# A hybrid encoder layer with routed experts: router product in column groups, and the order of work around the routing

## Chip, core and metric

The kernel runs on one core of a Trainium2 chip. The metric is the device time of one launch in microseconds (us), as the median of several runs. TensorE, VectorE, ScalarE, GpSimd and SyncE (which here only issues transfers) each run a stream of their own and are ordered by semaphores. Every tensor is float32.

## What is computed

Two sequences (256 and 1024 tokens, width 1024) go through two layers with shared weights. Each layer adds a mix of windowed attention, a bidirectional state space scan and a bidirectional mLSTM, and then a mixture of 16 experts, in which each expert chooses its tokens. The change touches the part from the output projection to the first expert:

```python
x = x + jnp.concatenate([ya, yb, yc], axis=-1) @ w_out[l]
h = _rmsnorm(x, ffn_norm[l])
aff = jax.nn.softmax((xf @ router).astype(jnp.float32), axis=-1)   # (T, 16)
gate, idx = lax.top_k(aff.T, cap)          # cap = 128 (sample), 32 (prompt)
xs = xf[idx]
hid = jax.nn.silu(einsum('ecd,edf->ecf', xs, w_gate)) * einsum('ecd,edf->ecf', xs, w_up)
ye = einsum('ecf,efd->ecd', hid, w_down) * gate[..., None]
out = zeros.at[idx.reshape(-1)].add(ye.reshape(-1, D))
```

## The kernel before, in words

The 1280 tokens are 10 blocks of 128 (`NC`), taken in `ORDER`: the eight of the sample first, then the two of the prompt (`NP`). A loop over layers (`Fori`) holds one block in which each engine's program is written out by hand; the order of lines is the order of work on that engine. A helper (`link`) adds a semaphore step to an instruction and has its own engine wait for it, so VectorE and ScalarE run strictly one instruction after the other. On TensorE all products go through `mm` (L1474) and on VectorE most operations through `tt` and `ts` (L984, L988), so rows are told apart by their tiles and shapes. A float32 product is two records in the trace.

**The passes.** TensorE runs `for n in range(1, NC + 1)` (L1870 on). Pass n makes the output projection of block n in two halves of eight products each (`out_proj(n, hf, i0, i1)`: 128x512, the weights of w_out moving), and in between the attention of later blocks (`scores`, `turn_p`, `turn_y`), the transposes of the normalized block n-1 (`turn_h2`, into PSUM bank 3) and its router product (`logits`, L1820). VectorE adds the projection to x (`add_x`), copies the transposed halves to `H2T` (`keep_h2`, for the last two blocks on ScalarE), and makes a softmax of the logits in two steps: `route_shift` (maximum and subtraction) and, after ScalarE's exponential `route_exp`, `route`. ScalarE also squares x, scales it by the root that GpSimd makes, and takes the attention's exponentials (`attn_exps`). The eight products of `logits` have a block of H2T (128x128) stationary and 16 columns of the router moving.

**The rounds.** When the eight sample blocks are routed, TensorE transposes their affinities into bank 7 (`aff_turned`, L1907), VectorE copies them to `AFF` (32 rows, one per expert and half of the sequence, 512 columns) and takes the eight best of every row 16 times (`best_eight`: MAX8, FIND_INDEX8, MATCH_REPLACE8; `rounds(lo, hi)`). The last two blocks (prompt) are still being projected meanwhile, and their adds, shifts and scalings are set between the rounds by hand. The last four rounds take the prompt's 16 rows too, after a second turn of affinities.

**Towards the experts.** `top_done` lets TensorE turn the lists so that each partition has its token's index; `keep_clock(6, 8)` issues eight products that nobody reads; GpSimd gathers the prompt's tokens of four experts (`gather_quad(0)`) and the sample's of the first (`gather(0)`), TensorE transposes them (`turn_quad`, `turn_tokens`), and VectorE copies them with the norm's gain into `XT` (`copy_quad`, `spread_quad`, `copy_tokens`; `g_copied` counts the half blocks). Then the loop over e starts with `EG` and `EU` (gate and up).

**SyncE's queue.** After the last stores it issues `down_load(0)`, then for e from 1 `gate_up_load(e)` and `down_load(e)`; each of these is 2 MB a tensor, and from e = 2 on they wait for the buffer of expert e-2.

**Parameters** sit in one tile `part`, in the order of the table `PAR`; `router` is 8 x 16 columns and stands last. `FOLD` (made on VectorE at the start of a layer, L1013) has 32 columns; column e sums the partitions p with p mod 32 = e. It is used by the gates of the mixers, whose products already stand in four column groups.

## Time and profile before

| what | us |
|---|---|
| runs | 2566.73, 2566.39, 2561.0 |
| median | 2566.39 |
| profiled execution | 2561.19 |
| its span in the trace | 2559.5 |
| TensorE busy | 2393.1 (93%) |
| VectorE busy | 1041.7 (41%) |
| ScalarE busy | 560.6 (22%) |
| GpSimd busy | 528.4 (21%) |

The span runs from the first to the last instruction of the profiled execution; the time around it is 1.7 us. The shares are means over stages that have different limits. A layer takes roughly half of the span, and its passes lie at 600 to 780 us and 1870 to 2050 us, the rounds at 780 to 821 and 2051 to 2092, the experts behind them. A row of a timeline has the start, the time, engine, line, operation, tiles, shape and count, and in brackets the idle time before it with what ended it. Matmul records overlap, so the start of the next row, not the sum of durations, tells what a group costs.

### The profile page before, as it was taken

To read this page: it belongs to the slowest core of one execution; us is meant where nothing else is said; L and a number is where in the kernel's file an instruction comes from. 1 tells how busy PE (TensorE), PEld (TensorE's weight loads), DVE (VectorE), ACT (ScalarE), POOL (GpSimd) and SP (SyncE) were. 2 spreads that over 40 slices of the span, in tenths; PEclk is the share of its full clock that TensorE was granted. 3 is DMA by queue.
4 is the path that set the end of the run, shared out by engine and by line. 5 is a ranking of instruction groups with operands and counts; after the bars stand their busy time and mean duration, and the time that the engine had idled before them with its cause. 6 is when DMAs were issued, how large, how long until landed. Compare 5 with 4: busy or idle time off the path is not lost. (4 is left out here: it accounts for less than half of the span.)

```text
span 2559.5 us, 34127 instructions
## 1 busy us (share of the span) xinstructions
PE 2393.1 (93%) x13478; PEld 1733.6 (68%) x13478; DVE 1041.7 (41%) x1990; ACT 560.6 (22%) x1202; POOL 528.4 (21%) x544
## 2 busy tenths in 40 slices
PE   5999998998996999999869999999989969999997
PEld 3567577874554887887635675778745548878876
DVE  3672345487537111111138524455865371111111
ACT  3220223243331111111132202323333211111110
POOL 1002444143211111211110114531332001111111
PEclk8999999999997999999989999999999979999999
DMA  6010322121227687887331012211212276788782
GB/s 219 19 34 17 99 83 70 63 84 66 72 74 261 212 277 262 298 269 260 104 121 36 17 43 89 88 61 59 91 50 75 75 271 228 258 292 286 250 291 65
DMA packets 149654, 357.61 MB, mean 140 GB/s; under 512 B 9981, under 2 KB 38273, under 8 KB 149410
## 3 DMA queue, kind: packets, MB, share of 16 engines
q1 hardware_dynamic: 134514, 313.42, 34.4%
q0 software_dynamic: 14976, 41.95, 6.6%
q8 instruction: 110, 1.80, 0.3%
q14 instruction: 54, 0.44, 0.1%
HBM read 313.06 MB, written 47.52 MB: 141 GB/s over the span
## 5 line engine op out<-in xcount | busy, mean ns | idle before, releaser
L1474 PE MATMUL ps<-MID,HT 128*128 128x512 f32 (+1 forms) x2176 | 595.1, 495 | 4.3 <-PE ps L1474 3.2
L1474 PE MATMUL ps<-HT,MID 128*128 128x160 f32 (+1 forms) x4192 | 583.9, 307 | 7.2 <-DVE HT L984 2.9
L1474 PEld LDWEIGHTS ps<-HT,MID 128*128 128x128 f32 (+1 forms) x4192 | 563.0, 189 | 25.9 <-issue 25.6
L1474 PE MATMUL ps<-RING,HT 128*128 128x256 f32 (+2 forms) x2080 | 475.1, 397 | 9.3 <-ACT MID L791 4.6
L1474 PEld LDWEIGHTS ps<-RING,HT 128*128 128x128 f32 (+1 forms) x2080 | 377.1, 193 | 98.2 <-issue 43.8
L1474 PEld LDWEIGHTS ps<-MID,HT 128*128 128x128 f32 (+1 forms) x2176 | 231.5, 152 | 225.7 <-issue 209.2
L1474 PE MATMUL ps<-HT,RING 128*128 128x512 f32 (+1 forms) x960 | 354.1, 526 | 3.1 <-ACT MID L785 2.5
L993 DVE SCALAR_TENSOR_TENSOR HT<-HT,ps 128x160 f32<-128x160 f32 x128 | 41.1, 321 | 712.0 <-ACT HT L970 712.0
L1474 PEld LDWEIGHTS ps<-HT,RING 128*128 128x128 f32 x960 | 180.9, 191 | 164.1 <-issue 156.4
L741 POOL DMA_INDIRECT y_sample<-SCR,idxs x32 | 50.6, 1581 | 745.5 <-ACT SCR L977 745.5
L970 ACT ACTIVATE HT<-ps 128x160 f32<-128x160 f32 x128 | 38.9, 304 | 593.7 <-PE ps L1474 593.7
L984 DVE TENSOR_TENSOR HT<-ps,part 128x512 f32<-128x512 f32 (+1 forms) x180 | 113.7, 632 | 65.7 <-PE ps L1488 22.7
L608 POOL TENSOR_TENSOR SCR<-MID,small 128x512 f32<-128x512 f32 x32 | 39.7, 1242 | 344.6 <-DVE MID L984 274.3
L984 DVE TENSOR_TENSOR SCR<-SCR,ps 128x512 f32<-128x512 f32 x80 | 55.0, 687 | 130.6 <-POOL SCR L622 95.7
L1474 PE MATMUL ps<-MID 128*64 128x128 f32 (+3 forms) x1136 | 101.0, 312 | 4.4 <-DVE RING L988 2.3
L1474 PEld LDWEIGHTS ps<-MID 64*128 64x128 f32 (+1 forms) x1136 | 75.8, 175 | 36.8 <-issue 26.0
L984 DVE TENSOR_TENSOR SCR<-SCR,small 128x1024 f32<-128x1024 f32 (+1 forms) x60 | 59.3, 989 | 95.3 <-POOL SCR L617 94.7
L1474 PE MATMUL ps<-MID,SCR 128*128 128x65 f32 (+1 forms) x640 | 79.4, 277 | 11.7 <-DVE TMP L984 11.7
L975 ACT ACTIVATE SCR<-ps,small 128x512 f32<-128x512 f32 x64 | 44.0, 687 | 201.6 <-PE ps L1474 201.6
L1474 PEld LDWEIGHTS ps<-MID,SCR 128*128 128x128 f32 x640 | 74.4, 191 | 17.6 <-issue 14.8
L677 POOL TENSOR_TENSOR SCR<-SCR,small 128x1536 f32<-128x1536 f32 (+1 forms) x20 | 48.1, 2406 | 177.8 <-DVE small L1281 177.6
L984 DVE TENSOR_TENSOR TMP<-MID,small 128x256 f32<-128x256 f32 (+1 forms) x64 | 26.9, 420 | 140.3 <-PE ps L1474 139.2
(212 smaller groups left out, 2183.0 us busy)
## 6 DMA issues: line engine op xcount, KB each, us to landing
MID<-w_gate SPq DMA_DIRECT2D x32, 2048.0 KB, 8.6
MID<-w_up SPq DMA_DIRECT2D x32, 2048.0 KB, 14.1
MID<-w_down SPq DMA_DIRECT2D x32, 2048.0 KB, 14.7
RING<-w_in SPq DMA_DIRECT2D x22, 1024.0 KB, 5.3
SCR<-cs_rows SPq DMA_DIRECT2D x20, 1024.0 KB, 5.2
SCR<-m_rows SPq DMA_DIRECT2D x20, 512.0 KB, 4.0
MID<-y_sample SPq DMA_DIRECT2D x16, 512.0 KB, 7.6
MID<-w_out SPq DMA_DIRECT2D x8, 1024.0 KB, 6.4
```

Of the source, the lines that this page charges most:

```text
L608: link(pool.tensor_tensor(DXS[:, n % 2, d, :].rearrange("p (h e) -> p h e", h=SH), XS[:, c, :].rearrange("p (h e) -> p h e", h=SH), WS[:, ...
L677: link(pool.tensor_tensor(v, v, ADEN[n % 2].unsqueeze(2).to_broadcast([P, AH, nk * P]), ALU.mult), pn_made)
L741: pool.indirect_dma_start(ys[:, :], bass.IndirectOffsetOnAxis(ap=idxs[:, e:e + 1], axis=0), YO[e % 2], None, compute_op=ALU.add, bounds_ch ...
L970: link(act.activation(THG, ps[:, 2 + f % 2, 0:TOK], ACT.Tanh, scale=0.5), gate_tanh)
L975: link(act.mul(YO[e % 2][:, hf * 512:(hf + 1) * 512], ps[:, 4 + hf, :], gts[:, e:e + 1]), down_scaled)
L984: link(dve.tensor_tensor(out, a, b, op), to)
L993: link(dve.scalar_tensor_tensor(out=out, in0=a, scalar=x, in1=b, op0=op0, op1=op1), to)
L1474: return pe.matmul(out, a, b, start=start, stop=stop)
```

## The change

It has five parts.

1. `logits` has the router's columns stationary and H2T moving, product k in column group k mod 4 (32 columns each, the 16 of the router and 16 that follow it, so that `router` moves to the front of `PAR`). Four partial sums lie in 4 x 32 partitions. ScalarE copies them to the tile `LGP`, and `fold_logits` multiplies LGP with 16 columns of FOLD, which gives the logits in the old shape and place.
2. In the passes, `logits(n - 1)` stands ahead of `turn_y(n + 1, 2)`, the fold after the fifth product of the second half, and in pass 8 the last product of the projection comes after the transposes for AFF.
3. VectorE's rounds are cut into a pick and a drop, the add of block 8 goes behind the first pick, and the shifts and scalings of the prompt's blocks are placed anew. The memset of AFF's unused part is moved ahead of the passes.
4. SyncE waits for the first two gathers before `down_load(1)`.
5. `keep_clock` has five products for eight, and the first expert's first products start with half of the tokens' copies.

```diff
-for _name, _w in (("gmix", 8), ..., ("dskip", 8), ("router", 128)):
+for _name, _w in (("router", 128), ("gmix", 8), ..., ("dskip", 8)):
+ROUTER = PAR["router"][0]
+        LGP = VO[:, 1664:1664 + P]
@@ SyncE
                 for e in range(1, E):
                     gate_up_load(e)
+                    if e == 1:
+                        sp.wait_ge(quad_gathered[0], 16)
+                        sp.wait_ge(gathered[0], 16)
                     down_load(e)
@@ ScalarE
+                def keep_logits(c):
+                    act.wait_ge(lg_parts, c + 1)
+                    if c >= 1:
+                        act.wait_ge(lg_made, c)
+                    link(act.copy(LGP, ps[:, 3, 0:P]), lg_kept)
...
                     if n >= 1:
+                        keep_logits(n - 1)
                         route_exp(n - 1)
@@ VectorE
-                def best_eight(r):
+                def pick_eight(r):
+                    rows, v8, places = ranked(r)
                     link(dve.max(v8, rows))
-                    link(dve.max_index(idxus[0:n, 8 * r:8 * r + 8], v8, rows))
-                    if r < CAPS // 8 - 1:
-                        link(dve.match_replace(rows, v8, rows, -1.0))
+                    link(dve.max_index(places, v8, rows))
+                def drop_eight(r):
+                    rows, v8, places = ranked(r)
+                    link(dve.match_replace(rows, v8, rows, -1.0))
...
-                link(dve.memset(AFF[2 * E:3 * E, SEQS[0]:512], -1.0))
-                add_x(NC - 2, 1)
                 dve.wait_ge(aff_turned, 1)
                 link(dve.tensor_copy(AFF[0:2 * E, :], ps[0:2 * E, 7, :]))
-                rounds(0, 3)
+                pick_eight(0)
+                add_x(NC - 2, 1)
+                drop_eight(0)
+                rounds(1, 4)
                 take_x(NC - 1)
-                rounds(3, 5)
+                rounds(4, 6)
                 route_shift(NC - 2)
-                rounds(5, 6)
+                pick_eight(6)
                 route(NC - 2)
+                drop_eight(6)
                 add_x(NC - 1, 1)
-                rounds(6, 10)
+                rounds(7, 10)
+                pick_eight(10)
                 route_shift(NC - 1)
-                rounds(10, 11)
+                drop_eight(10)
                 route(NC - 1)
                 rounds(11, PROMPT_ROUND)
@@ TensorE
-                pe.wait_ge(fold_made, 1)
                 def logits(c):
                     pe.wait_ge(h2t_copied, 2 * c + 2)
                     for k in range(KD):
-                        last = mm(ps[:, 3, 0:E], H2T[:, k, :], pr("router")[:, k * E:(k + 1) * E], k == 0, k == KD - 1)
-                    last.then_inc(lg_made, 1)
+                        j = k % 4
+                        last = mm(ps[32 * j:32 * j + 32, 3, 0:P], part[:, ROUTER + k * E:ROUTER + (k + 2) * E], H2T[:, k, :], k < 4, k >= 4)
+                    last.then_inc(lg_parts, 1)
+                def fold_logits(c):
+                    pe.wait_ge(lg_kept, c + 1)
+                    mm(ps[:, 3, 0:E], LGP, FOLD[:, 0:E]).then_inc(lg_made, 1)
...
                     out_proj(n, 1, 1, 3)
+                    logits(n - 1)
                     if n + 1 < NC:
                         turn_y(n + 1, 2)
-                    out_proj(n, 1, 3, 4)
-                    logits(n - 1)
-                    out_proj(n, 1, 4, 8)
+                    out_proj(n, 1, 3, 5)
+                    fold_logits(n - 1)
+                    out_proj(n, 1, 5, 7)
                     if n == NC - 2:
                         pe.wait_ge(aff_made, NC - NP)
...
                         last.then_inc(aff_turned, 1)
+                    out_proj(n, 1, 7, 8)
...
-                keep_clock(6, 8)
+                keep_clock(6, 5)
...
-                    pe.wait_ge(g_copied, turn_at(e, 1) + 1)
+                    pe.wait_ge(g_copied, turn_at(e, 1) + (1 if e else 0))
...
                             for k in range(KD):
+                                if n == 0 and (at, k) == (0, KD // 2):
+                                    pe.wait_ge(g_copied, turn_at(0, 1) + 1)
```

## Rows read from the trace of the kernel before

**Rows 1.** Busy time by stretch (us, PE, PEld, DVE, ACT, POOL, clock, DMA share, GB/s), one pass.

```profile
712.70:733.68 20.98, 20.82 (x96) 11.16 (x95) 8.53 (x19) 6.71 (x18) 2.17 (x3) 1.00 0.21 75
```

**Rows 2.** Timeline, VectorE, rounds of layer 2: copy, two maxima, cast after the last.

```profile
2051.45 0.68 DVE L1399 COPY TMP<-ps 32x512 f32<-32x512 f32 x1
2052.16 0.68 DVE L1355 MAX8 TMP<-TMP 32x8 f32<-32x512 f32 x1
...
2054.44 0.68 DVE L1355 MAX8 TMP<-TMP 32x8 f32<-32x512 f32 x1
...
2091.82 0.17 DVE L1415 CAST TMP<-idxus 16x32 f32<-16x32 uint32 x1
```

**Rows 3.** Timeline, `keep_clock` in both layers, token copies and first expert product.

```profile
824.15 6.82 PE L1474 MATMUL ps<-cstt 128*128 128x384 f32 x16
...
2094.67 8.14 PE L1474 MATMUL ps<-cstt 128*128 128x384 f32 x16
...
2105.13 1.42 DVE L984 TENSOR_TENSOR HT<-ps,part 128x512 f32<-128x512 f32 x2
2106.65 14.95 PE L1474 MATMUL ps<-HT,MID 128*128 128x160 f32 x96 [1.17 <-issue]
```

**Rows 4.** Timeline of a pass in layer 1 around `logits`, all engines.

```profile
707.94 0.69 DVE L1337 COPY HT<-ps 128x512 f32<-128x512 f32 x1
...
708.27 1.88 PE L1474 MATMUL ps<-MID,HT 128*128 128x512 f32 x4
...
709.80 0.20 ACT L922 ACTIVATE small<-small 128x4 f32<-128x4 f32 x1
...
710.08 1.53 PE L1474 MATMUL ps<-MID 128*64 128x128 f32 x24
...
712.70 1.85 PE L1474 MATMUL ps<-part,HT 128*128 128x16 f32 x16
...
714.41 5.40 PE L1474 MATMUL ps<-MID,HT 128*128 128x512 f32 x12
...
726.76 0.37 ACT L930 COPY MID<-ps 128x256 f32<-128x256 f32 x1 [3.50 <-PE ps L1757]
```

**Rows 5.** Groups of TensorE records by shape, whole span: count | busy, mean ns.

```profile
L1474 PE MATMUL ps<-MID,HT 128*32 128x256 f32 x1024 | 61.9, 382 | 0.0
...
L1474 PE MATMUL ps<-MID 128*64 128x128 f32 x416 | 28.9, 289 | 2.3 <-DVE RING L988 2.3
```

**Rows 6.** Timeline, end of pass 8 in layer 1: routing, transposes, copy to AFF.

```profile
775.97 0.18 DVE L1342 TENSOR_REDUCE small<-ps 128x1 f32<-128x16 f32 x1 [2.42 <-PE ps L1474]
...
777.12 0.23 DVE L988 TENSOR_SCALAR TMP<-MID,small 128x16 f32<-128x16 f32 x1
...
779.23 0.60 PE L1907 MATMUL ps<-cstt,TMP 128*32 128x128 f32 x4
...
780.23 0.68 DVE L1399 COPY TMP<-ps 32x512 f32<-32x512 f32 x1
```

**Rows 7.** Timeline, layer 1: the last add, the last logits, the last shift.

```profile
796.34 0.69 DVE L984 TENSOR_TENSOR RING<-ps,RING 128x512 f32<-128x512 f32 x1
...
803.26 3.59 PE L1474 MATMUL ps<-part,HT 128*128 128x16 f32 x16 [0.75 <-ACT HT L935]
...
806.96 0.17 DVE L1342 TENSOR_REDUCE small<-ps 128x1 f32<-128x16 f32 x1 [0.82 <-PE ps L1474]
```

**Rows 8.** First gathers: two issues (timeline), then their time to landing (transfers by window).

```profile
825.67 0.96 POOL L717 DMA_INDIRECT HT<-h_sample,idxs  x1 [0.85 <-DVE idxs L984]
...
2094.11 1.08 POOL L723 DMA_INDIRECT HT<-h_prompt,idxg  x1 [23.63 <-DVE idxg L1421]
...
HT<-h_sample,idxs POOLq DMA_INDIRECT x1, 5.0
...
HT<-h_prompt,idxg POOLq DMA_INDIRECT x1, 4.4
```

**Rows 9.** Busy time by stretch as in rows 1, one microsecond after expert 0's start.

```profile
2107.00:2108.00 1.00, 1.00 (x6) 1.00 (x5) 0.00 (x0) 0.00 (x0) 0.00 (x0) 0.50 0.07 16
```

More of the change, by code:

```diff
@@ L27 @@
 _n = 0
-for _name, _w in (("gmix", 8), ("gffn", 8), ("gy", 8), ("convw", 30), ("convb", 6), ("qg", 1), ("kg", 1),
-                  ("sink", 4), ("gbias", 32), ("alog", 16), ("dskip", 8), ("router", 128)):
+for _name, _w in (("router", 128), ("gmix", 8), ("gffn", 8), ("gy", 8), ("convw", 30), ("convb", 6), ("qg", 1), ("kg", 1),
+                  ("sink", 4), ("gbias", 32), ("alog", 16), ("dskip", 8)):
     PAR[_name] = (_n, _n + _w)
@@ L343, in program @@
         scaled_odd = layer_sem("scaled_odd")
-        fold_made = layer_sem("fold_made")
         softplus_exp = layer_sem("softplus_exp")
@@ L410, in program @@
         lg_made = layer_sem("lg_made")
+        lg_parts = layer_sem("lg_parts")
+        lg_kept = layer_sem("lg_kept")
         h2t_copied = layer_sem("h2t_copied")
@@ L1009, in scale_x @@
                     ts(XN[c], XN[c], rs[:, c:c + 1], None, ALU.mult, to=scaled_odd)
-                link(dve.tensor_reduce(out=FOLD, in_=ident.rearrange("p (j e) -> p e j", j=4), axis=AX, op=ALU.add), fold_made)
+                link(dve.tensor_reduce(out=FOLD, in_=ident.rearrange("p (j e) -> p e j", j=4), axis=AX, op=ALU.add))
                 ts(NSINK, pr("sink"), -1.0, None, ALU.mult)
@@ L1349, in route, with ranked @@
                     ts(AFTM[:, j, g * E:(g + 1) * E], AFT, rec[:, 0:1], None, ALU.mult, to=aff_made)
-                def best_eight(r):
+                def ranked(r):
                     n = 3 * E if r >= PROMPT_ROUND else 2 * E
-                    rows, v8 = AFF[0:n, :], VALS[0:n, 8 * r:8 * r + 8]
+                    return AFF[0:n, :], VALS[0:n, 8 * r:8 * r + 8], idxus[0:n, 8 * r:8 * r + 8]
+                def pick_eight(r):
+                    rows, v8, places = ranked(r)
                     link(dve.max(v8, rows))
-                    link(dve.max_index(idxus[0:n, 8 * r:8 * r + 8], v8, rows))
-                    if r < CAPS // 8 - 1:
-                        link(dve.match_replace(rows, v8, rows, -1.0))
+                    link(dve.max_index(places, v8, rows))
+                def drop_eight(r):
+                    rows, v8, places = ranked(r)
+                    link(dve.match_replace(rows, v8, rows, -1.0))
                 def rounds(lo, hi):
                     for r in range(lo, hi):
-                        best_eight(r)
+                        pick_eight(r)
+                        if r < CAPS // 8 - 1:
+                            drop_eight(r)
                 def take_x(n):
@@ L1374, in _ @@
                 attn_den(2)
+                link(dve.memset(AFF[2 * E:3 * E, SEQS[0]:512], -1.0))
                 for n in range(1, NC - 1):
```

## Prediction

> **What bounds the kernel now.** I read three views in this order. The busy table by stretch comes first, for one pass of the loop over n: TensorE works 20.82 of 20.98 us at the full granted clock of 1.00, that is at 2.4 GHz, while VectorE has 8.53 and ScalarE 6.71 [rows 1]. So the passes are bound by TensorE, and what it sheds there is gained one for one. The timeline of the routing stretch comes second. From the copy into AFF to the cast after the last round VectorE takes 2091.82 - 2051.45 = 40.37 us in layer 2. One round lasts 2054.44 - 2052.16 = 2.28 us and there are 16, the last without its replace [rows 2]. 15 x 2.28 + 1.5 = 35.7, and the copy, three adds at 0.72, two shifts and two scalings fill the rest, so this stretch is bound by VectorE and moves only with its start. The timeline behind it comes third: `keep_clock`, four transpose blocks, VectorE's scaling copies, and the first expert product at 2106.65 [rows 3]. From there the expert loop is TensorE's alone, and the change leaves it as it is. A microsecond gained ahead of it is a microsecond of the end.
>
> **Logits in column groups.** Old: 16 records from 712.70 to 714.41, 1.71 us, 0.107 each [rows 4]. New: 16 records with 32 columns stationary and 128 moving, four groups side by side. No row has this shape. The nearest is the down projection of the prompt, also four groups, with 256 moving columns: 61.9 / 1024 = 0.060 us a record; two groups with 128 moving take 28.9 / 416 = 0.069 [rows 5]. The latter bounds the new block above at 1.11 us. Below, half of 0.060 for half the columns gives 0.48. I take 0.60, near the four-group row, with something for starting up. The fold is one product of two records with a full stationary matrix, 2 x 0.107 = 0.21, and the additional block boundary costs up to 0.1 (the two-group block starts at 710.08 where 708.27 + 4 x 0.427 = 709.98 was due) [rows 4]; I take 0.09. A pass saves 1.71 - 0.60 - 0.21 - 0.09 = **0.81 us**, between 0.29 and 0.93.
>
> The Trainium skill ("TensorEngine Tiling (Array Packing)", Key Properties) says that changing the tiling mode drains TensorE. That speaks against this change, which adds such switches in every pass. The 0.10 before the two-group block is a price for one switch; the rule would make it up to a full drain both ways, which is rival B.
>
> **What hides the new steps.** `logits` now stands before the last `turn_y`, at about 709.98 instead of 712.70. It waits for the second half of H2T, copied by 707.94 + 0.69 = 708.63, so it isn't late. The new ScalarE copy of 128 columns is shorter than the 0.37 us one of 256 [rows 4]; I take 0.28. ScalarE's exponentials of the pass end at 710.00, the logits at 710.6, so the copy is done by 711.1. TensorE has the last `turn_y` (1.53 us and more) and two out_proj products (4 x 0.427 = 1.71) before the fold waits at about 713.9: 2.8 us of cover. In the passes with three key blocks ScalarE's end moves by some 0.4 us only. Behind the copy on ScalarE stands only `route_exp`, which needs the fold anyway. Without this cover a pass would lose the 0.5 us from the end of the logits to the end of the copy. `lg_made` stays where it was in the pass to 0.1 us, so routing isn't later.
>
> **End of the eighth pass.** One of the four last out_proj products now comes after the four transposes for AFF: 2 x 0.427 = 0.85 us earlier. They wait for `route(7)`: its chain takes 777.12 + 0.23 - 775.97 = 1.38 us from the logits [rows 6], and two products, 1.71 us, now cover it; before there were four. It just fits. Old, the transposes ended at 779.83 but VectorE copied at 780.23, behind add_x(8, 1); that add now stands behind the first pick, so the copy starts up to 0.30 us sooner. VectorE's chain starts 8 x 0.81 + 0.85 + 0.30 = **7.6 us earlier** in each layer. The memset that is moved up lies in idle time: nothing.
>
> **The chain of rounds.** It now contains add_x(8, 1): +0.72, 41.1 us without stalls. Does a stall come with the new order? add_x(9, 1) now stands behind the copy, picks and drops of 0 to 6, two adds, a shift and a scaling, at S + 19.0 (S is the chain's start), old at 796.34 - 780.23 = S + 16.1 [rows 6, 7]. TensorE's half for it is ready at about S + 17.5: ScalarE's square of row block 8 starts 1.8 us later against TensorE's pass, which holds `turn_h2(8, 0)` up by some 1.5 us, all inside this slack. From add_x(9, 1) to the last shift it took 806.96 - 796.34 = 10.6 us, of which the slow logits took 3.59, being at 1.2 GHz, and VectorE stood still for 0.82 [rows 7]. New, logits, copy and fold take some 2.5, so 9.5 us: the fold ends near S + 28.5, where VectorE arrives at S + 28.1. I put a stall of 0.4 in layer 1, and none in layer 2, where VectorE was kept busy and TensorE was partly at the full clock. Layer 1 exchanges 0.82 - 0.1 of old stall for 0.4, net cost 0.72 - 0.3 = 0.4; layer 2 pays 0.72. Top_done comes 7.2 and 6.9 us earlier, **14.1 together**. For the stall the bounds are 0 and 1.2 us a layer.
>
> **keep_clock 8 to 5.** Six records fewer. The 16 took 8.14 us in layer 2 and 6.82 in layer 1 [rows 3]. At full clock one is three times a 128-column record, 0.32 us, at half clock 0.64; so 9.4 of them ran at half clock in layer 2, 5.3 in layer 1, and in both the last six were fast. Dropping six saves 6 x 0.32 = 1.9 us, if what follows is ready. The quad gather is issued at 2094.11 and lands 4.4 us later, 2098.5, and the product would end at 2100.9; in layer 1 the same gather has 4.4 us from a similar place. The token gather is issued at about 825.67 and lands 5.0 us later, 830.7 [rows 8]; `turn_tokens(0, 0)` would come at about 830.4 in layer 1: up to 0.3 us short. This is what the **new wait on SP** is for. down_load(1), 2 MB, used to travel in the same time as the gathers; now it is issued after both landed. Behind it on SP stands only gate_up_load(2), which waits for expert 0's gate and up anyway, 20 us later, and down_load(1) is wanted some 40 us later, with 14.7 us to landing in the median. So the wait costs nothing, and it gives the gathers some of the 0.3. I take 1.9 in both layers.
>
> The Trainium skill ("DMA: Bandwidth & Descriptors", Issuing engines are not separate DMA queues) says that transfers of all issuing engines interleave on the same 16. No row separates how much the gathers lose to the weights; by that rule the wait can only bring them forward.
>
> **First product of expert 0** no longer waits for the second half of the tokens: VectorE's two copies are 1.42 us from 2105.13, the first ends at 2105.84, and the product started at 2106.65, 0.10 behind the second [rows 3]. New 2105.94: **0.7 us a layer**. The other four k wait after 8 records, longer than one copy, so covered.
>
> Reordered parameters are one DMA of the same size, and the dropped fold_made wait is nothing, as FOLD is made long before.
>
> **Sum.** 14.1 + 2 x 1.9 + 2 x 0.7 = **19.3 us**. The profiled execution has a span of 2559.5 and took 2561.2 us; it gives 2541.9. It stands 5.2 us under the median of the runs, 2566.4, which gives 2547.1. The runs lie at both levels, so I take 2546.
>
> **Rivals.**
> A: *the clock or a gather takes the tail's gain.* In layer 2 the granted clock fell to 0.50 (1.2 GHz) at 2107, just as expert 0 began, after the transposes with their idle time [rows 9]; that cost about 1.6 us for 3.2 us at half rate. With fewer warm products ahead, it may fall in both layers, or rise later, and the gathers may bind: 2 to 6 us lost, 2548 to 2552. For it: the fall in layer 2. Against: layer 1 kept the clock, and the idle time gets shorter. 0.15.
> B: *the groups share less than the four-group row says, or each switch drains.* At the two-group price the block is 1.11: 0.51 x 16 = 8 us less, 2554. A full drain is about 0.17 us (four transposes take 0.60 where their pitch makes 0.43) [rows 6], 0.24 more a pass, 3.8 us less, 2550. Against it: 0.060 at double the columns. 0.08.
> C: *slower than before.* It is one mechanism: the four groups run one after the other, at 0.107 us a record as full-width ones do. The block stays at 1.71, and fold and switches add 0.21 + 0.44, so a pass loses 0.65 instead of gaining 0.81, 23.4 us in 16 passes: 2546 + 23.4 = 2569 to 2570. It is slower from the point where the block costs more than about 1.8 us, with the tail's gain counted. The 0.060 record, a third of the 0.213 that 256 columns take alone, nearly excludes it. 0.01.
> D: *the DVE chain hides the passes' gain*, or the fold waits for ScalarE each pass: 2555 to 2560. [rows 1] and the 2.8 us of cover speak against it. 0.03. That the change does not do what it says in the rows (the copy finds no gap and is later than the fold) is this case.
> Forecast: 0.73, with 2539 to 2549 for it alone.
>
> The range is 2538 to 2555: it takes in A and B, the low level of the runs, and block prices to 1.11. A measurement of this kernel tells about 0.3%, 7.7 us, from no change, so faster needs under 2558.7: 0.95; same 0.04; slower 0.01.
>
> **What the profile would show.** The logits as 16 records within 0.5 to 0.7 us, a ScalarE copy of 128 x 128, a fold of 2 records without idle time before it; passes of 20.2 instead of 20.98 us; the AFF copy 7.6 us earlier in layer 1; the rounds 41.1 to 41.5 us; keep_clock of 10 records with next to no idle time before the quad's transposes; the first expert product 0.1 us behind the first token copy. I am wrong if the block takes over 0.9 us, if VectorE waits over 1 us at the last shift, or if the clock is at 1.2 GHz for expert 0 in both layers.

## The result, and the profile after

The changed kernel takes 2536.32 us (2532.66 to 2539.33, four runs), the one before 2566.56 in the same job (four runs). The ratio is 0.9886 with a 95% interval of 0.9865 to 0.9907. A second job with five runs of the changed kernel gave 2533.77 beside 2562.76 us for the kernel before (20 runs), ratio 0.9886, interval 0.9868 to 0.9903. That is 29 to 30 us where I forecast 20, and 2536.3 lies under my range of 2538 to 2555. In one of the experiments below one of four executions took 3587 us at a mean granted clock of 0.65 and is left out of its median.

The profiled execution has a span of 2536.8 us. I cut both executions into ten stages: in each layer the mixers (to the first shift of the routing), the passes (to the copy for AFF), the rounds (to the cast after the last), the way to the first expert product, and the experts. These are the rows of busy time by stage of the kernel after, with the columns of [rows 1]:

```profile
0.00:629.61 629.61, 578.02 (x2923) 407.28 (x2924) 336.95 (x566) 176.33 (x357) 165.73 (x186) 0.96 0.22 74
629.61:775.39 145.78, 144.67 (x732) 74.68 (x731) 68.61 (x141) 49.51 (x126) 26.76 (x32) 1.00 0.21 76
775.39:816.46 41.07, 20.86 (x88) 10.12 (x86) 38.86 (x91) 8.09 (x16) 1.48 (x4) 0.78 0.81 296
816.46:827.48 11.02, 9.56 (x58) 7.00 (x59) 5.16 (x19) 0.00 (x0) 4.97 (x5) 0.73 0.68 226
...
1288.62:1886.12 597.50, 564.18 (x2908) 399.78 (x2907) 335.11 (x564) 170.15 (x349) 162.34 (x167) 0.98 0.19 63
1886.12:2031.90 145.78, 144.66 (x732) 74.67 (x731) 68.59 (x142) 49.51 (x126) 26.75 (x32) 1.00 0.21 76
2031.90:2072.98 41.08, 20.86 (x88) 10.12 (x86) 38.87 (x92) 8.09 (x16) 1.48 (x4) 0.78 0.82 296
2072.98:2085.41 12.43, 11.25 (x59) 7.63 (x59) 5.15 (x19) 0.00 (x0) 4.85 (x5) 0.64 0.72 241
2085.41:2536.80 451.39, 436.88 (x2960) 356.28 (x2960) 71.00 (x180) 49.04 (x112) 65.34 (x47) 0.99 0.72 242
```

and the same stages of the kernel before (layer 1, then layer 2 without its mixers):

```profile
0.00:625.38 625.38, 571.55 (x2919) 404.05 (x2920) 336.99 (x565) 176.03 (x356) 165.65 (x186) 0.97 0.22 75
625.38:780.23 154.85, 153.74 (x723) 84.02 (x722) 70.66 (x144) 47.64 (x119) 26.80 (x32) 1.00 0.20 72
780.23:821.30 41.07, 22.18 (x82) 13.35 (x80) 38.20 (x90) 7.55 (x14) 1.49 (x4) 0.74 0.90 326
821.30:834.81 13.51, 11.60 (x64) 8.04 (x65) 5.78 (x19) 0.00 (x0) 4.99 (x5) 0.79 0.82 292
...
1896.61:2051.45 154.84, 153.73 (x723) 84.01 (x722) 70.64 (x144) 47.63 (x119) 26.80 (x32) 1.00 0.20 72
2051.45:2091.82 40.37, 21.31 (x82) 12.64 (x80) 38.20 (x90) 7.55 (x14) 1.49 (x4) 0.77 0.90 325
2091.82:2106.65 14.83, 12.92 (x65) 8.68 (x65) 5.77 (x19) 0.00 (x0) 4.86 (x5) 0.72 0.80 284
2106.65:2559.50 452.85, 438.55 (x2960) 357.95 (x2960) 70.33 (x179) 49.04 (x112) 65.40 (x47) 0.98 0.70 236
```

The second and third numbers are what to look at: the length of the stage and TensorE's busy time in it. The passes lose 9.07 us in each layer, and TensorE's busy time in them falls by the same 9.07. The rounds do not move in layer 1 and are 0.7 us longer in layer 2. The way to the first product is 2.4 to 2.5 us shorter. The mixers, which the change does not touch, are 4.2 us *longer* in layer 1 of this execution, and 2.8 us shorter in layer 2 (597.5 us, before 600.3).

A pass in the timeline of the kernel after, where [rows 4] answers:

```profile
728.96 1.88 PE L1498 MATMUL ps<-MID,HT 128*128 128x512 f32 x4
...
730.77 0.64 PE L1498 MATMUL ps<-HT,part 128*32 128x128 f32 x16
...
731.35 1.09 PE L1498 MATMUL ps<-MID 128*64 128x128 f32 x16
731.53 0.27 ACT L948 COPY MID<-ps 128x128 f32<-128x128 f32 x1 [0.60 <-PE ps L1498]
...
732.60 1.96 PE L1498 MATMUL ps<-MID,HT 128*128 128x512 f32 x4 [0.16 <-PE ps L1498]
...
733.96 0.19 PEld L1498 LDWEIGHTS ps<-small,MID 128*128 128x128 f32 x1 [0.24 <-issue]
734.39 0.29 PE L1498 MATMUL ps<-small,MID 128*128 128x16 f32 x2
734.53 3.68 PE L1498 MATMUL ps<-MID,HT 128*128 128x512 f32 x8
```

From start to start the logits take 731.35 - 730.77 = 0.58 us for 16 records, the fold 734.53 - 734.39 = 0.14, with no idle time ahead of it: the copy ended at 731.80. The fold's first weight load (PEld, 733.96) lies under the wide product ahead of it. Around the two grouped blocks there are two small gaps. The four wide records before them take 730.77 - 728.96 = 1.81 us and the four behind them 734.39 - 732.60 = 1.79, where 4 x 0.427 = 1.71 is their pitch. That is 0.08 to 0.10 us for each change between full-width and grouped products. In the kernel before, the group of `turn_y` has the same two (the first is the 0.10 of the prediction, and two records from 711.77 to 712.70 take 0.93 for 0.85). The logits stand right against `turn_y`, so they add none, and none is to be seen between their four groups and its two.

The end of pass 8, where [rows 6] answers, and the last add, logits and shift, where [rows 7] answers, in layer 1:

```profile
774.29 0.23 DVE L1001 TENSOR_SCALAR TMP<-MID,small 128x16 f32<-128x16 f32 x1
774.69 0.60 PE L1937 MATMUL ps<-cstt,TMP 128*32 128x128 f32 x4
...
775.39 0.68 DVE L1418 COPY TMP<-ps 32x512 f32<-32x512 f32 x1 [0.87 <-PE ps L1937]
...
781.81 0.66 PE L1840 MATMUL ps<-cstt,HT 128*128 128x128 f32 x4 [1.37 <-ACT HT L966]
...
794.45 0.69 DVE L997 TENSOR_TENSOR RING<-ps,RING 128x512 f32<-128x512 f32 x1
...
801.37 1.08 PE L1498 MATMUL ps<-HT,part 128*32 128x128 f32 x16 [0.75 <-ACT HT L941]
...
802.88 0.61 PE L1498 MATMUL ps<-small,MID 128*128 128x16 f32 x2 [0.43 <-ACT MID L948]
803.59 0.17 DVE L1355 TENSOR_REDUCE small<-ps 128x1 f32<-128x16 f32 x1
```

The copy now waits for the transposes themselves and not for an add. The last shift has 0.1 us of idle time ahead of it (it had 0.82 us), so in layer 1 the add that was put into the chain is paid by a stall that went.

The way to expert 0 in layer 1, where [rows 3] and [rows 8] answer:

```profile
819.31 4.98 PE L1498 MATMUL ps<-cstt 128*128 128x384 f32 x10
...
820.83 0.95 POOL L723 DMA_INDIRECT HT<-h_sample,idxs  x1 [0.85 <-DVE idxs L997]
...
824.12 1.04 PE L1968 MATMUL ps<-cstt,HT 128*128 128x128 f32 x8
...
825.93 1.09 PE L1976 MATMUL ps<-cstt,HT 128*128 128x128 f32 x8 [0.77 <-DMA HT<-h_sample,idxs]
...
827.48 7.71 PE L1498 MATMUL ps<-HT,MID 128*128 128x160 f32 x55 [0.46 <-issue]
```

Here TensorE waits 0.77 us for the token gather. That is so in one of the four cases (two layers in each of two executions of the changed kernel); in the other three it waits 0.51 us for VectorE's copy, as before the change. The start of the quad's transposes splits the way; this is the row of the kernel before in layer 1, and that of the changed kernel in layer 2:

```profile
830.81 1.04 PE L1937 MATMUL ps<-cstt,HT 128*128 128x128 f32 x8
```

```profile
2082.13 1.04 PE L1968 MATMUL ps<-cstt,HT 128*128 128x128 f32 x8
```

From these transposes to the first expert product it takes 4.00 us before (834.81 - 830.81, and 4.00 to 4.01 in all six cases) and 3.28 after (2085.41 - 2082.13); with the gather's wait it is 3.36. So the wait of 0.77 us costs 0.1. From the start of `keep_clock` to the transposes it takes 6.66 to 8.17 us before, 7.20 in the mean, and 4.81 to 6.30 after, 5.74 in the mean.

### The profile page after: what moved, and what is told of

Same layout as the page of the kernel before. It is cut to its first block and busy times, and to the rows that moved or that the text cites. A ratio compares the mean times of both kernels' runs of the same rounds, so it can differ in the third digit from the quotient of the medians.

```text
span 2536.8 us, 34223 instructions
## 1 busy us (share of the span) xinstructions
PE 2369.3 (93%) x13506; PEld 1705.3 (67%) x13506; DVE 1039.3 (41%) x1990; ACT 565.9 (22%) x1222; POOL 527.8 (21%) x544
## 5 line engine op out<-in xcount | busy, mean ns | idle before, releaser
L1498 PEld LDWEIGHTS ps<-HT,MID 128*128 128x128 f32 (+1 forms) x4192 | 561.1, 188 | 23.4 <-issue 23.2
L1006 DVE SCALAR_TENSOR_TENSOR HT<-HT,ps 128x160 f32<-128x160 f32 x128 | 41.1, 321 | 708.8 <-ACT HT L983 708.8
```

Of the source, the lines that this page charges most:

```text
L1006: link(dve.scalar_tensor_tensor(out=out, in0=a, scalar=x, in1=b, op0=op0, op1=op1), to)
L1498: return pe.matmul(out, a, b, start=start, stop=stop)
```

## The experiments

All kernels but the two repeats of the kernel before are edits of the changed kernel.

**Repeats.** What part of the difference is the change, and what part scatter.

> The changed kernel, unedited, beside five rounds of the kernel before. Question: the two profiled executions differ by 22.7 us of span, the two medians by 30.2 us. Theory 1 (the change is worth what its own stages show): passes 9.1 us a layer, rounds 0 and -0.7, from the rounds' end to the first expert product 2.4 a layer, some 24 us in all, and the other 6 us are scatter of stages that the change doesn't touch, in both kernels. Then the ratio of this run lies near 0.9905 within its interval, and the mixer stages of this execution (start to the first routed block) differ from those of the first one by microseconds in either direction. Rival (the change also speeds up a stage it doesn't touch, for instance by the new place of the parameters): ratio below 0.9890, and both mixer stages shorter than before's 594.6 and 600.3 us.

Measured: 2533.77 us, ratio 0.9886 (0.9868 to 0.9903). The stages are those of the first execution: passes 145.78 in both layers, rounds 41.08 in both, way to the first product 12.10 and 12.00. Mixers 630.1 and 596.3. The ratio is that of the first job, and the 0.9905 that I wrote down for theory 1 lies just outside its interval. The rival's mark fails too: the mixers of layer 1, from FOLD to the first shift, take 598.4 us and not under 594.6.

> The kernel before, unedited: how far its stages repeat from one execution to the next. Scatter theory: the two mixer stages (start to first shift: 625.4; FOLD to first shift in layer 2: 600.3 us in the first profile) move by 2 to 6 us, while passes (150.6 us from the first to the eighth shift), rounds (41.1 and 40.4) stay within 0.1 us. Rival: the stages all repeat within 0.5 us, and the 6 us must come from the change.

Measured: 2562.48 us (2557.16 to 2566.76, ten runs), ratio 1.0001 (0.9986 to 1.0016). Mixers 626.8 and 598.5, passes 154.85 in both layers, rounds 41.06 and 41.07, way 13.65 and 13.66. So the 40.37 us of layer 2's rounds, on which I had built, was one execution's: there TensorE had the full clock for the last transposes (eight records in 1.09 us), here it had not, and VectorE waited as in layer 1. The rows of this execution:

```profile
2071.64 1.97 PE L1817 MATMUL ps<-cstt,HT 128*128 128x128 f32 x8 [4.31 <-ACT HT L954]
...
2078.07 0.17 DVE L1342 TENSOR_REDUCE small<-ps 128x1 f32<-128x16 f32 x1 [0.82 <-PE ps L1474]
```

> The kernel before once more, for the scatter. Theory (scatter sits in the two mixer stages): their sum is within 1219 to 1230 us as in all kernels so far, passes 154.85 us, rounds 41.1 or 40.4, rounds' end to first expert product 13.5 to 14.9. Rival (the change makes the mixer stages shorter): their sum is above 1226 here again and the mean of the three executions of this kernel lies 3 us over that of the others.

Measured: 2562.49 us (ten runs), ratio 1.0011 (0.9995 to 1.0026). Mixers 628.8 and 596.9, passes 154.85, rounds 41.07 and 41.07, way 13.65 and 15.02, the last just over what I had written. The sum of the two mixer stages is 1225.6, 1225.3 and 1225.7 us in the three executions of the kernel before. In the eleven of the changed kernel and its variants it is 1219.7 to 1229.6, 1225.7 in the mean. So no effect of the change on them is to be seen, and they carry microseconds of scatter from one execution to the next. Passes and rounds repeat to 0.1 us, but for the 40.37 us of one layer. The experts of layer 1 move between 460.3 and 461.7 us in all fourteen executions, and the way to the first product moves with the clock. In the six executions with five products in `keep_clock` and SyncE's wait it takes 11.00 to 12.51 us, and nearly all of that is how long the ten records of `keep_clock` take. So a difference of some tenths in this stage between two runs says nothing.

**Column groups against the old product.**

```diff
                     for k in range(KD):
-                        j = k % 4
-                        last = mm(ps[32 * j:32 * j + 32, 3, 0:P], part[:, ROUTER + k * E:ROUTER + (k + 2) * E], H2T[:, k, :], k < 4, k >= 4)
-                    last.then_inc(lg_parts, 1)
+                        last = mm(ps[:, 3, 0:E], H2T[:, k, :], part[:, ROUTER + k * E:ROUTER + (k + 1) * E], k == 0, k == KD - 1)
+                    last.then_inc(lg_made, 1)
...
-                        keep_logits(n - 1)
-                    fold_logits(n - 1)
```

> The changed kernel with the router product as before (block of H2T stationary, 16 columns moving, no copy, no fold), at the new place in the pass. Theory (the column groups and the fold give the passes' gain, 0.98 us a pass): a pass is 0.98 us longer than the changed kernel's, the stage from the first shift to the copy for AFF 7 x 0.98 = 6.9 us longer in each layer, and the time 14 to 18 us above the changed kernel (a little more for the slow logits at the end of the rounds, if VectorE then waits). Rival (the gain is in the order, since the move of the product shortened a wait on TensorE): less than 0.5 us a pass, under 8 us in all.

Measured: 2555.8 us (eight runs), ratio 0.9965 (0.9948 to 0.9983), 22 us above the changed kernel of the same job. Busy time by stage, passes and rounds of layer 1, and the end of the rounds in the timeline:

```profile
627.83:780.75 152.92, 151.81 (x720) 84.49 (x719) 66.31 (x142) 47.65 (x119) 26.80 (x32) 1.00 0.20 73
780.75:823.30 42.55, 23.55 (x84) 13.77 (x82) 38.89 (x91) 7.55 (x14) 1.48 (x4) 0.75 0.82 296
```

```profile
810.43 0.17 DVE L1354 TENSOR_REDUCE small<-ps 128x1 f32<-128x16 f32 x1 [1.59 <-PE ps L1497]
```

The passes are 152.92 - 145.78 = 7.1 us longer in each layer, near the 6.9 of the theory. But it is eight passes of 0.89 us (22.50 to 21.61 us for a whole one) and not seven of 0.98. The rounds are 1.5 us longer too, because the slow logits at the low clock (3.59 us, as in [rows 7]) come 1.59 us late for VectorE. The groups give 2 x (7.1 + 1.5) = 17 us of the gain. The medians say 22, more than the 14 to 18 that I expected; the other 5 us are in no stage of the profiled execution. And 154.85 - 152.92 = 1.9 us of the passes' 9.1 are the order's: 0.85 for the last product, the rest from the add that the copy no longer follows and from a pass that got shorter by 0.09 (22.60 to 22.51 us) by the new place of the product alone.

**The cover of the copy.**

```diff
-                    logits(n - 1)
                     if n + 1 < NC:
                         turn_y(n + 1, 2)
-                    out_proj(n, 1, 3, 5)
+                    out_proj(n, 1, 3, 4)
+                    logits(n - 1)
                     fold_logits(n - 1)
+                    out_proj(n, 1, 4, 5)
```

> The changed kernel with logits at its old place (after the fourth product of the second half) and the fold right behind it. Theory (the cover of the ScalarE copy matters): TensorE waits in each pass for the copy, 0.27 us and the two semaphore steps, about 0.5 to 0.7 us a pass, 16 passes, 8 to 11 us slower than the changed kernel. Rival (ScalarE's copy is late anyway or TensorE drains as long without it): within 3 us of the changed kernel.

Measured: 2546.17 us (five runs), ratio 0.9936 (0.9914 to 0.9958), 12.4 us above the changed kernel. The passes are 151.37 us, 5.6 longer in each layer, 0.70 a pass. The timeline shows where:

```profile
713.43 1.10 PE L1498 MATMUL ps<-MID,HT 128*128 128x512 f32 x2 [0.16 <-PE ps L1498]
714.46 0.65 PE L1498 MATMUL ps<-HT,part 128*32 128x128 f32 x16
...
715.21 0.27 ACT L948 COPY MID<-ps 128x128 f32<-128x128 f32 x1 [3.54 <-PE ps L1498]
...
715.53 0.39 PE L1498 MATMUL ps<-small,MID 128*128 128x16 f32 x2 [0.43 <-ACT MID L948]
...
715.77 5.40 PE L1498 MATMUL ps<-MID,HT 128*128 128x512 f32 x12
```

From the logits' start to the fold's start it is 1.07 us where the logits alone take 0.58: 0.49 us of the 0.70 are the wait for the copy. The rest is in the rows around it. The fold takes 715.77 - 715.53 = 0.24 us for 0.14, now that it comes straight behind the grouped logits with its weight load uncovered. And the logits no longer stand against `turn_y`: the two wide records between them take 714.46 - 713.43 = 1.03 us, where in [rows 4]'s pass they take 0.93. So uncovered, most of the 0.89 us that the groups give a pass is gone.

**The order at the end of the eighth pass** (`out_proj(n, 1, 5, 8)` ahead of the transposes; VectorE's sequence as before).

> The changed kernel with the old order at the end of the eighth pass: the last product ahead of the transposes, the add of block 8 ahead of the copy for AFF, the old places of shifts and scalings between the rounds. Theory (VectorE's chain moves only with its start): the stage from the first shift to the copy is 0.85 to 1.2 us longer in each layer, the rounds are 40.3 us if VectorE never waits, 0.7 shorter than the 41.08 of the changed kernel, so 0.1 to 0.5 us a layer slower, under 1 us in all, which the times can't tell. Rival (with the add back ahead of the copy the logits of the last block come in time, and the rounds have no stall at all, while in the changed order they have): rounds below 40.2, and this order is the faster one by up to 0.5 us a layer. Rival 2: VectorE waits at the last shift with the old places, since the chain there is now shorter but so is its cover: rounds above 41.

Measured: 2538.5 us (four runs), ratio 0.9905 (0.9883 to 0.9927). Passes 146.92 (1.14 longer), rounds 40.24 and 40.23 (0.84 shorter), the same in both layers. Together 0.3 us a layer. The mechanism is as expected: the chain starts later and is shorter. So the new order of instructions at the end of the pass brings 0.6 us in both layers, too little for the times to tell.

**keep_clock with eight products.**

> The changed kernel with eight products in keep_clock, as before. Theory (keep_clock stands on the path to the first expert product): the stage from the rounds' end to the first expert product gets 1.1 to 2 us longer in each layer (12.0 on average in the changed kernel, 13.1 to 14 here), the six records more at 0.32 us each less what the token gather hides; 2 to 4 us in all. Rival (the gathers bound it before the change as well): within 0.5 us a layer. Rival 2 (the short keep_clock costs clock): the granted clock of the stage is higher here and the first expert products come no later than in the changed kernel.

Measured: 2538.52 us (four runs), ratio 0.9912 (0.9892 to 0.9931). The way to the first product:

```profile
810.74:825.11 14.37, 13.19 (x64) 8.78 (x65) 5.15 (x19) 0.00 (x0) 4.97 (x5) 0.69 0.76 256
2069.51:2082.57 13.06, 11.88 (x65) 8.14 (x65) 5.16 (x19) 0.00 (x0) 4.86 (x5) 0.76 0.73 243
```

13.7 in the mean against 11.02, 12.43, 12.10 and 12.00 us of the changed kernel, 1.8 us a layer, and both are longer than any of the twelve ways with five products (11.00 to 12.51). keep_clock is on the path.

**keep_clock with three.**

> The changed kernel with three products in keep_clock. Theory (from five on the gather bounds it, not keep_clock): the rounds' end to the first expert product is 11.0 to 11.5 us in both layers, whatever the clock does. Rival (clock): the transposes and the start of expert 0 run at 1.2 GHz; the granted clock in the first 10 us of expert 0 is below 0.9 in one layer or both, and what is gained in the stage is lost again behind it.

Measured: 2534.79 us (four runs), ratio 0.9894 (0.9868 to 0.9919). The way in layer 1, the first 13 us of expert 0 behind it, and the way in layer 2:

```profile
816.36:826.95 10.59, 9.47 (x54) 6.70 (x55) 5.15 (x19) 0.00 (x0) 4.98 (x5) 0.62 0.65 210
826.95:840.00 13.05, 13.05 (x96) 13.05 (x97) 2.20 (x6) 0.61 (x2) 0.00 (x0) 1.00 0.56 227
2072.25:2082.88 10.63, 9.42 (x54) 6.95 (x55) 5.15 (x19) 0.00 (x0) 4.86 (x5) 0.61 0.68 226
```

10.6 us in both, below every way with five products and below the 11.0 at which I had the gather bind. In layer 1 the token transposes wait for VectorE's copy (0.45 us), in layer 2 for the gather (0.53). The quad's transposes themselves ran at the low clock in part (1.60 and 1.71 us for 1.04), and yet expert 0 has the full clock from its start in both layers. Whether keep_clock is needed at all was not tried.

**SyncE's wait** (the three lines taken out).

> The changed kernel without SyncE's wait before expert 1's down weights. Theory (the wait brings nothing): the gathers landed 4.4 and 5.0 us after their issue with the weights' transfer beside them and 5.1 and 4.9 without, so the first expert product comes at the same time within 0.3 us. Rival (the wait was what let keep_clock be shortened): the token gather lands 0.5 us or more later, and TensorE stands still before turn_tokens by that much.

Measured: 2536.96 us (four runs), ratio 0.9904 (0.9879 to 0.9929). The way takes 12.25 and 12.29 us, against 12.10 and 12.00 in the repeat. TensorE waited 0.30 us for the quad's gather in layer 2, which it did not do in the changed kernel, and not at all for the tokens. But the transfers changed more than the way did. The row of the way in layer 1, and the landing of the first gather there:

```profile
815.38:827.63 12.25, 11.06 (x59) 7.38 (x59) 5.16 (x19) 0.00 (x0) 4.98 (x5) 0.66 1.03 408
```

```profile
HT<-h_prompt,idxg POOLq DMA_INDIRECT x1, 6.5
```

The DMA engines are busy without a break (1.03, against 0.68 in the changed kernel). The first gather lands 6.5 and 6.6 us after its issue in the two layers, where it takes 4.3 to 4.5 in the two executions of the changed kernel; the token gather lands after 5.7 and 5.8 us, there after 4.7 to 5.5. So the half us that the rival put on the token gather is there, and TensorE's wait for it is not. It costs little because `keep_clock` ran mostly at the low clock in this execution and covered it: the quad's transposes start 8.9 and 9.0 us after the rounds' end. Where they start at 7.7, as in layer 1 of the changed kernel, the quad's tokens would land at 2.3 + 6.5 = 8.8, so by these rows I estimate the wait at up to 1.2 us there. The theory's comparison was empty: in the kernel before, the weights' loads began 20.8 us after the copy for AFF and were over when the gathers moved, and with the changed order they begin 23.8 us after it.

**The first expert product waiting for both halves** (`turn_at(e, 1) + 1` for all e, inner wait out).

> The changed kernel with the first expert product waiting for both half blocks of tokens, as before. Theory: 0.7 us longer between the last transposes and the first expert product in each layer (start 1.15 us after the end of the transposes instead of 0.45), 1.4 us in all, not to be told by the times. Rival (the second wait inside the first eight products costs the same): the two kernels reach the second group of products at the same time.

Measured: 2540.15 us (four runs), ratio 0.9919 (0.9895 to 0.9944). The product starts 1.17 us behind the end of the transposes, in the changed kernel 0.44 to 0.46. That is 0.7 us a layer, as expected, and the inner wait costs nothing behind it: the experts of layer 2 take 451.23 and 451.39 us. The stage as a whole took 11.95 and 11.84 us, no longer than the changed kernel's mean, because `keep_clock` took only 5.1 and 5.0 us from start to transposes in this execution (5.74 in the mean of the changed kernel), the clock having risen earlier. The median is higher than the 1.4 us explain; I count that as scatter and can't show it.

**A version meant to beat both.** The copy for the fold was done 0.8 us ahead of the end of `turn_y` (731.80 against 732.60), so the fold can come one product earlier, and with it routing, and in pass 8 the transposes:

```diff
-                    out_proj(n, 1, 3, 5)
+                    out_proj(n, 1, 3, 4)
                     fold_logits(n - 1)
-                    out_proj(n, 1, 5, 7)
+                    out_proj(n, 1, 4, 6)
...
-                    out_proj(n, 1, 7, 8)
+                    out_proj(n, 1, 6, 8)
```

> The changed kernel with the fold one product earlier in each pass (after the fourth product), and in pass 8 the transposes after the sixth product, two products behind them. The copy for the fold is done 0.8 us before the last turn_y ends, so nothing should wait. Theory (VectorE's chain hangs on the transposes): the copy for AFF comes 0.85 us earlier, the rounds stay at 41.1 or get up to 0.5 us longer, because the last blocks' projections end later against the rounds; net 0.4 to 0.85 us a layer faster, 1 to 1.7 us in all, in the stages; the times can barely tell it. Rival: VectorE waits at the shift of block 8 or 9 for as much as was gained; rounds 41.9.

Measured: 2537.52 us (the median of three runs), ratio 0.9900 (0.9871 to 0.9929). Passes 144.92, 0.86 shorter in both layers, rounds 41.08 in both: 1.7 us by the stages, hidden in the scatter of the times.

> The version meant to beat both: the changed kernel with the fold one product earlier and keep_clock of four products. Theory: the copy for AFF 0.86 us earlier in each layer (as in the run with the early fold alone), and where the clock is still low during keep_clock, the quad's transposes start up to 1.3 us earlier (two records of 0.64), bounded by the token gather, which lands some 9.3 us after the rounds' end: first expert product 11.0 to 11.4 us after the rounds' end instead of 11.0 to 12.5. 1.7 to 3 us under the changed kernel in all. Rival (fewer warm products bring the low clock into expert 0): the stage gets shorter, but the first expert's products run at 1.2 GHz for some microseconds, 1.5 us or more lost, and the time is that of the changed kernel.

Measured: 2532.42 us (2531.97 to 2532.82, four runs), ratio 0.9888 (0.9863 to 0.9912). The passes of layer 1 and the way to the first expert product in both:

```profile
627.20:772.12 144.92, 143.81 (x730) 74.28 (x729) 68.54 (x142) 49.50 (x126) 26.80 (x32) 1.00 0.21 77
...
813.19:824.10 10.91, 9.37 (x57) 6.77 (x57) 5.15 (x19) 0.00 (x0) 4.98 (x5) 0.69 0.66 218
...
2068.56:2079.67 11.11, 9.93 (x56) 6.92 (x57) 5.15 (x19) 0.00 (x0) 4.86 (x5) 0.66 0.67 221
```

It has the lowest median of all. The 2 x 0.86 = 1.7 us of the passes repeat the run before. The way is 11.01 us in the mean against 11.89 of the changed kernel, which would be another 1.8 us, but variants with five products reach 11.00 too, so how much of that is the fourth product and how much the clock isn't shown. The intervals of the two ratios overlap almost wholly, so the gain over the changed kernel rests on the passes alone.

## Why the prediction was right or wrong

The sign and the mechanism were right, and the size too small: 19.3 us worked out, 29 to 30 between the medians. None of the signs of being wrong that I had named came (a block over 0.9 us, a wait over 1 us at the last shift, a low clock in both layers). The step of the sum that failed is the saving of a pass: 0.81 us forecast, 0.99 measured. By its own steps:

- **TensorE bounds the passes**: right. Its busy time and the stage shrank by the same 9.07 us.
- **The pass**: 0.81 forecast, 0.99 measured (21.61 for 22.60 us, 19.99 for 20.98), above the upper bound of 0.93. The block was right (0.58 for 0.60), and so the two-group price is out. The fold takes 0.14, not 0.21: I priced both its records at the pitch of full-width ones in a row, but the first weight load lies beneath the wide product ahead of it. And the additional boundary that I priced at 0.09 does not exist: the logits stand against `turn_y`, and a pass has two changes between full-width and grouped products, as before. 1.71 - 0.58 - 0.14 = 0.99. Eight passes: 1.4 us a layer, 2.9 in all.
- **The end of pass 8**: 0.85 + 0.30 forecast; 9.07 - 8 x 0.99 = 1.15 measured. The transposes did not wait for routing: it was done at 774.52, and they started at 774.69, when the product ahead of them was through.
- **The rounds**: 41.1 to 41.5 us forecast, 41.07 and 41.08 measured, with a stall of 0.1. The step that failed is the comparison: I charged layer 2 with 0.72 because of the 40.37 us of one execution. In the two others, and in layer 1 always, the old rounds have the 0.82 us stall and 41.07 us. The net cost is 0 to 0.7, on average 0.13 a layer, and I had 1.1 in all: 0.9 us. The 1.5 us by which `turn_h2(8, 0)` was to be held up is 1.37, and harmless as said. My list of what fills the chain had three adds; the rows of the kernel before have two (787.78 and 796.34) and the copy of the prompt's affinities.
- **keep_clock and the first product**: 2.6 us a layer forecast. The means of the way are 14.05 us in the three executions of the kernel before and 11.89 in the two of the changed kernel, 2.2 a layer. The part behind the quad's transposes is as forecast (4.00 to 3.28, 0.72 for 0.7). The part before them is 7.20 - 5.74 = 1.46, not 1.9: I took away six fast records, but by 0.32 and 0.64 us a record 6.5 of the 16 were slow in the mean before, and 7.9 of the 10 after. In the variants the same ten records are often faster, so this is the scatter of the clock and no loss that the change is shown to make. It takes 0.9 us from the sum. The gather of which I had feared 0.3 binds in one case of four and costs 0.1.
- **SyncE's wait**: right that it costs nothing, but I gave it a wrong reason. In the kernel before, the weights were not beside the first gathers. With the changed order they would be, and the gather lands 2.1 us later beside them.
- **The clock (rival A)** went the other way at expert 0. The low clock at the start of layer 2's expert 0 [rows 9] was there in two of three executions of the kernel before (452.85 and 452.99 us for the experts of layer 2 against 451.44) and in none of the changed kernel and its variants (451.03 to 451.39). Where it was there, the way before it had been the long one, 14.8 and 15.0 us. On average that is 1.0 us gained, for which I had only a loss in the list. Why it went is open. With the gap of 1.17 back, both layers still had the full clock, and so had layer 1 of keep_eight, whose way was 14.4 us long with a gap of 0.44. So neither alone brings it in these runs.
- **The sum** by the means of the stages is 18.1 (passes), -0.3 (rounds), 4.3 (way), 1.1 and 0.1 (experts): 23.4 us, of which my terms held 19.3. The 4.1 more are 2.9 from the passes, 0.9 from the rounds and 1.2 from the experts, less 0.9 on the way. They alone would have left the time inside my range. The times say 24.9 to 33.8 in the second job. Over all runs in this document the means are 2562.3 (64 runs of the kernel before) and 2535.7 (nine of the changed kernel), 26.6 apart, so 3.2 us are in no stage that I can name, and 6.8 (30.2 less 23.4) by the medians of the forecast's job. The cause of that part stays open. The mixers are equal in the mean of the profiled executions, but they move between 1219.7 and 1229.6 us, and the executions that make the medians were not profiled. The two profiled ones of the changed kernel lie 2 to 4 us above its medians and the three of the kernel before 1 to 5 below theirs.
- **The base**: 2546 is a base of 2565.3 less 19.3. Over its 64 runs the kernel before has a mean of 2562.3, so 3.0 us of my miss come from there. The range was worked from the bounds of the terms and the level of three runs; it did not allow for a base that scatters by 4 us on its own, though the three runs shown already differed by 5.7.
- Rivals C and D did not occur, and B did not either, but the changed kernel does not test its second half, the drain. It has no more changes between full-width and grouped products than the kernel before. The variant with the logits at their old place has two more in a pass, and there each costs about 0.1 us (1.03 for 0.93, and 0.24 for 0.14 at the fold, where the uncovered weight load may have a part). The Trainium skill says that a change of tiling mode drains TensorE ("TensorEngine Tiling (Array Packing)", Key Properties). These 0.1 us agree with it, at less than the 0.17 of rival B. The Trainium skill states that transfers from all engines run on the same 16 DMA engines ("DMA: Bandwidth & Descriptors", Issuing engines are not separate DMA queues). The runs agree: the first gather takes 6.5 us beside the weights and 4.4 without.

## What to carry to other kernels

Here a matrix product with 16 output columns is cheaper with these columns stationary in four groups than with the wide side stationary (0.58 and 0.14 us for 1.71), even with a copy and a fold behind it; but the copy must lie behind other work of TensorE, or 0.7 of the 0.99 us is lost again. Put a grouped block against another grouped block, and price a moved block with the boundary it leaves as well as the one it makes. Before a stage's time is taken as the base of a sum, look whether it repeats in the other layer: at 40.37 against 41.07 us one layer had been spared a stall by luck. And when the order on one engine moves, look what transfers then run beside each other that did not before.

## What the runs showed that was not expected

- Two records with 16 moving columns between wide products take 0.14 us of TensorE, start to start, where such records in a row take 0.107 each.
- At the granted clock of 0.50 (1.2 GHz) the same 16 records of four groups take 1.08 us, where the wide ones take 3.59: the order of the advantage is kept when the clock is low.
- With three products instead of eight ahead of the transposes the granted clock was 0.62 and 0.61 in the stage and yet 1.00 from the first expert product on.
- A gather lands after 6.5 us beside a weights' load and after 4.4 without, and the stage around it is hardly longer, as long as TensorE is busy with `keep_clock` for that time.
- The two mixer stages scatter by up to 6 us (623.9 to 630.1 us in layer 1) while the passes repeat to 0.01 us.
